# Expert weights in 32 KB runs, two slots of four matrices, and the overflow path ahead of the last four experts

## What is computed

```
# per layer: 32 experts in 4 groups of 8; each token takes the best group and the 2 best experts in it
h2 = modulate(rms_norm(x), shift, scale)
y_e = (silu(h2 @ w_gate[e]) * (h2 @ w_up[e])) @ w_down[e]     # 1024 -> 512 -> 1024, float32
x = x + gate2 * sum over the token's 2 experts of weight * y_e
```

## Time and profile before

| | us |
|---|---|
| median of 3 runs | 2081.34 (2080.13 to 2082.64) |
| the profiled execution, its own time | 2077.69 |
| its span | 2075.9 |
| PE busy, share of the span | 1665.3, 80% |
| DMA, mean rate over the span | 281 GB/s |

### The profile page before, as it was taken

How to read it: one execution, slowest core, us unless ns; L and a number is a source line. 1 busy time by engine, 2 the same in 40 slices (tenths; PEclk the granted TensorE clock), 3 DMA queues, 4 the chain that set the end, 5 groups by cost and what they waited for, 6 DMA issues and landing times.

```text
span 2075.9 us, 26940 instructions
## 1 busy us (share of the span) xinstructions
PE 1665.3 (80%) x12123; PEld 1166.5 (56%) x12123; DVE 521.1 (25%) x931; ACT 323.4 (16%) x641; POOL 50.2 (2%) x79
## 2 busy tenths in 40 slices
PE   8998999999999975565565599999999666565566
PEld 6875877887888832222222188878887222222223
DVE  5776863523101220000000035231023000000001
ACT  2332313212211110000000142211001000000001
POOL 0011100100000000000000001000000000000000
PEclk9999999999999987887887899999999887787787
DMA  7798835204347489999999922134473999999995
GB/s 256 257 350 326 317 150 193 82 3 162 122 162 289 157 337 428 427 427 428 425 424 428 376 94 83 43 122 162 148 302 118 424 427 428 428 427 425 426 427 210
DMA packets 107975, 582.39 MB, mean 281 GB/s; under 512 B 13496, under 2 KB 16336, under 8 KB 83152
## 3 DMA queue, kind: packets, MB, share of 16 engines
q1 hardware_dynamic: 92560, 530.17, 63.3%
q0 software_dynamic: 13056, 50.33, 6.4%
q10 hardware_dynamic: 2240, 0.11, 0.1%
HBM read 579.54 MB, written 1.05 MB: 280 GB/s over the span
## 4 chain that ended last, share of the span: by engine, by line
PE 59%; DMA 23%; DVE 1%; ACT 1%; issue 1%
PE ps L2470 21%; PE ps L1316 13%; PE ps L2104 8%; DMA more_slots<-in_w_exp_up 5%; DMA ring<-in_w_exp_down 4%; DMA more_slots<-in_w_exp_down 4%; PE ps L2117 4%; DMA more_slots<-in_w_exp_gate 4%; DMA ring<-in_w_exp_gate 3%; DMA ring<-in_w_exp_up 3%; PE ps L2142 3%; PE ps L1319 1%; PE ps L1772 1%; PE ps L1784 1%; PE ps L1534 1%; PE ps L1790 1%
## 5 line engine op out<-in xcount | busy, mean ns | idle before, releaser
L2470 PE MATMUL ps<-more_slots,gathered 128*32 128x512 f32 x1184 | 286.7, 718 | 137.9 <-DMA ring<-in_w_exp_up 62.4
L2470 PE MATMUL ps<-ring,gathered 128*32 128x512 f32 x864 | 235.7, 731 | 118.8 <-DMA more_slots<-in_w_exp_up 78.2
L1316 PE MATMUL ps<-h,ring 128*128 128x256 f32 x1216 | 275.5, 382 | 0.0
L1316 PEld LDWEIGHTS ps<-h,ring 128*128 128x128 f32 x1216 | 227.5, 190 | 37.0 <-issue 4.5
L2568 DVE TENSOR_TENSOR gate_up_rows<-silu_rows,ps 128x512 f32<-128x512 f32 x16 | 11.0, 688 | 791.0 <-PE ps L2470 791.0
L2470 PEld LDWEIGHTS ps<-more_slots,gathered 128*32 128x32 f32 x1184 | 70.3, 129 | 247.2 <-issue 246.9
L2470 PE MATMUL ps<-more_slots,gate_up_turned 128*32 128x512 f32 x608 | 147.3, 740 | 70.0 <-DMA ring<-in_w_exp_down 54.1
L2470 PEld LDWEIGHTS ps<-ring,gathered 128*32 128x32 f32 x864 | 56.9, 131 | 208.7 <-issue 208.7
L2104 PE MATMUL ps<-h,ring 128*128 128x256 f32 x768 | 166.7, 379 | 0.0
L2470 PE MATMUL ps<-ring,gate_up_turned 128*32 128x512 f32 x416 | 128.5, 741 | 36.4 <-DMA more_slots<-in_w_exp_down 36.4
L2104 PEld LDWEIGHTS ps<-h,ring 128*128 128x128 f32 x768 | 145.9, 190 | 19.8
(11 more groups left out here) (470 smaller groups left out, 1824.0 us busy)
## 6 DMA issues: line engine op xcount, KB each, us to landing
more_slots<-in_w_exp_gate SPq DMA_DIRECT2D x40, 2048.0 KB, 18.1
more_slots<-in_w_exp_down SPq DMA_DIRECT2D x38, 2048.0 KB, 17.0
more_slots<-in_w_exp_up SPq DMA_DIRECT2D x34, 2048.0 KB, 15.2
ring<-in_w_in SPq DMA_DIRECT2D x31, 2048.0 KB, 9.1
ring<-in_w_exp_up SPq DMA_DIRECT2D x30, 2048.0 KB, 14.6
ring<-in_w_exp_down SPq DMA_DIRECT2D x26, 2048.0 KB, 15.2
ada_ring<-in_w_ada POOLq DMA_DIRECT2D x48, 1024.0 KB, 7.4
ring<-in_w_exp_gate SPq DMA_DIRECT2D x24, 2048.0 KB, 17.8
```

The lines of the kernel that those rows point to most:

```text
L1316: ins = nc.tensor.matmul(k.ps[:, IN_BANK[t], 0:S], slab[:, j, c:c + w], k.h[:, j, :], start=j == 0, stop=j == ND - 1)
L2470: ins = nc.tensor.matmul(k.ps[r, bank, :], left[:, j, r], slab[:, j, c0:c0 + 512], start=j == 0, stop=j == steps - 1)
```

## The change

1. **Layout.** The host stores the gate and up matrices as (layer, partition, expert, 4096), and the down matrices as (layer, column half, partition, expert, 2048). A load takes half a group, 4 MB, with 32 KB on each partition in one run: two experts of gate or up (neighbouring partitions lie 512 KB apart in memory), or one column half of all four downs (256 KB apart).
2. **Slots.** Two slots of four slabs (`expert_slots`, 64 KB per partition each) take the place of seven single ones. Group `g` waits until group `g - 2` is used. One gate slab and the whole up group are loaded ahead of `w_o`, the other three gate slabs as the ring comes free; the ring lies in the upper part of one expert slot. So eight slabs are there before the first group is used.
3. **Downs by column parts.** The left half has its own loads to wait for (`loaded`), the right half a semaphore of its own (`down_right`).
4. **Router weights by quads.** `weigh` (two DVE instructions of 128 columns) multiplies a quad's selection in place, PE turns it with two transposes (`turn_weights`), DVE copies it.
5. **The general path** is called ahead of quad 7 on all four engines, on SP ahead of group 21, and rebuilt (`rest_loads`, `rest_products`, `rest_activations`, `rest_sums`). The function table for the next norm is loaded behind the last SiLU.

```diff
-        for s in range(MORE):
-            load_expert(s)
+        load_gate(0)
+        for part in range(2):
+            load_half(1, part)
         for i in range(N_MIX - 2, N_MIX):
             left(i - SLOTS)
             load(i)
-        for i, s in enumerate(RING_ORDER):
+        for i in range(SLOTS):
             left(N_MIX - SLOTS + i)
-            load_expert(s)
-        for s in range(E_SLOTS, N_SLABS):
-            sp.wait_ge(sem.slabs_used, past.slabs_used + (s - E_SLOTS) // QUAD + 1)
-            load_expert(s)
+            load_gate(1 + (N_MIX * (l + 1) + i) % SLOTS)
+        for g in range(2, N_GROUPS):
+            if g == N_GROUPS - 3:
+                rest_loads(k, y, sp)
+            sp.wait_ge(sem.groups_used, past.groups_used + g - 1)
+            for part in range(2):
+                load_half(g, part)
...
+            if q == N_QUAD - 1:
+                rest_products(k, y, pe)
...
             pe.wait_ge(sem.gu_t_ready, past.gu_t_ready + q + 1)
-            four(1, gu_t, s + 2 * QUAD, 0, N_F).then_inc(sem.down_done, 1)
-            four(0, gu_t, s + 2 * QUAD, 512, N_F).then_inc(sem.slabs_used, 1)
-            if q == 0:
-                pe.wait_ge(sem.scatter_ready, past.scatter_ready + 2)
+            loaded(3 * q + 2)
+            four(1, gu_t, down[:, 0], 0, N_F).then_inc(sem.down_done, 1)
+            pe.wait_ge(sem.down_right[l], 16 * (q + 1))
+            four(0, gu_t, down[:, 1], 0, N_F).then_inc(sem.groups_used, 1)
+            pe.wait_ge(sem.scatter_ready, past.scatter_ready + q + 1)
             scatter_rows(q)
...
             nc.scalar.activation(act_buf[:, :], k.ps[:, 0, :], ACT.Silu).then_inc(sem.act_done, 1)
+            if q == N_QUAD - 1:
+                nc.scalar.preload_act_table_set("natural_log_exp_and_others")
...
         for i in range(SLOTS):
             if l:
-                sp.wait_ge(sem.slabs_used, past.slabs_used - (i < SLOTS - 1))
+                sp.wait_ge(sem.groups_used, past.groups_used - 1)
             load(i)
...
-            remaining_experts(k, y, block)
```

More of the change, by code:

```diff
@@ L1196, in first_block, with expert_rows, group_slot @@
     k.clear(one + ring)
[L1199 to L1218, removed]
+N_GROUPS = 3 * N_QUAD
+def expert_rows(io, l, q, n, part):
+    if n < 2:
+        rows = io[("w_exp_gate_2", "w_exp_up_2")[n]][l, :, q * QUAD + 2 * part:q * QUAD + 2 * part + 2, :]
+    else:
+        rows = io["w_exp_down_2"][l, part, :, q * QUAD:(q + 1) * QUAD, :]
+    return rows.rearrange("p e c -> p (e c)")
+def group_slot(k, g):
+    return k.slots[:, (g + 1) % 2, :]
 N_IN = 11
@@ L2196, in _ @@
                                 ).then_inc(sem.token_sum, 1)
[L2199 to L2209, removed]
-    loaded = (rest.gate_loaded, rest.up_loaded, rest.down_loaded)
[L2212 to L2236, removed]
-            for t in range(NT):
[L2238 to L2252, removed]
@@ new lines, in rest_products @@
+def rest_products(k, y, pe):
+    nc, sem, past, rest = k.nc, y.sem, y.past, y.sem.rest[y.l]
+    h2, gu = k.h2, k.rest_gu
+    loaded = (rest.gate_loaded, rest.up_loaded, rest.down_loaded)
+    with overflow(k, y, pe):
+        pe.wait_ge(sem.rows_left, past.rows_left + N_QUAD)
+        pe.wait_ge(sem.rows_right, past.rows_right + N_QUAD)
+        for t in range(NT):
+            ins = nc.tensor.transpose(k.ps[:, 0, t * P:(t + 1) * P], k.rest[:, t, :], k.const("ident"))
+        ins.then_inc(rest.products, 1)
+        pe.wait_ge(rest.sums, 1)
+        for j in range(ND):
+            for t in range(NT):
+                ins = nc.tensor.transpose(k.ps[:, j // 2, (2 * (j % 2) + t) * P:(2 * (j % 2) + t + 1) * P],
+                                          k.h2_tok[:, t, j, :], k.const("ident"))
+        ins.then_inc(rest.products, 1)
+        with pe.Fori(0, N_E) as e:
+            pe.wait_ge(rest.sums, e * 2 + 2)
+            for n in range(2):
+                pe.wait_ge(loaded[n], e * 16 + 16)
+                slab = k.ring[:, n, :].rearrange("p (j c f) -> p j f c", j=ND, f=N_F)
@@ L2253, in _ @@
                 for f in range(N_F):
                     for j in range(ND):
[L2255 to L2271, removed]
@@ new lines, in rest_products @@
+                        ins = nc.tensor.matmul(k.ps[:, 2 * n + f // 2, f % 2 * S:(f % 2 + 1) * S],
+                                               slab[:, j, f, :], h2[:, j, :], start=j == 0, stop=j == ND - 1)
+            ins.then_inc(rest.products, 1)
+            pe.wait_ge(rest.sums, e * 2 + 4)
+            pe.wait_ge(loaded[2], e * 32 + 32)
+            slab = k.ring[:, 2, :].rearrange("p (b f j c) -> p b f j c", b=2, f=N_F, c=P)
+            for f in range(N_F):
+                for j in range(ND):
+                    ins = nc.tensor.matmul(k.ps[:, 4 + j // 2, j % 2 * S:(j % 2 + 1) * S],
+                                           slab[:, j // 4, f, j % 4, :], gu[:, f // 2, f % 2, :],
+                                           start=False, stop=True, skip_group_check=True)
@@ L2425, in router_rest @@
     step(nc.vector.tensor_tensor(weight[:, :, :], chosen[0][:, :, :], chosen[1][:, :, :], ALU.add))
-    last = lambda a: a.rearrange("p (e o) -> p e o", o=1).broadcast_to([P, N_E, CAP])
-    dve.wait_ge(sem.picked, past.picked + N_QUAD)
-    for t in range(NT):
-        ins = nc.vector.tensor_tensor(k.pick_w[:, t, :, :], k.pick[:, t, :, :], last(weight[:, t, :]), ALU.mult)
     dve.wait_ge(sem.zeros, past.zeros + 2)
@@ L2559, in take_rows, with weigh @@
             ins.then_inc(sem.rows_left, 1)
+        def weigh(q):
+            es = slice(q * QUAD, (q + 1) * QUAD)
+            for t in range(NT):
+                by = k.weight[:, t, es].rearrange("p (e o) -> p e o", o=1).broadcast_to([P, QUAD, CAP])
+                ins = nc.vector.tensor_tensor(k.pick[:, t, es, :], k.pick[:, t, es, :], by, ALU.mult)
+            ins.then_inc(sem.weighted, 1)
         take_rows(0)
```

220 lines of the change are left out of this document (130 added, 90 removed).

## The result

The changed kernel takes 2049.64 us (median of 4 runs, 2048.19 to 2051.91), the one before 2081.77 beside it (4 runs, 2080.13 to 2082.64): ratio 0.985, 95% interval 0.9836 to 0.9863. That is 32.1 us less. The forecast was 2049.8.

What follows compares the result with a forecast made beforehand. Expert phases were taken as bound by their DMA transfers. Terms 9.8 (slabs), 7.0 (downs), 8.2 (branch) make 25.0 us, 31.5 with the rate's 6.5: from the median 2081.3 to 2049.8 us, range 2040 to 2066.

Steps and rivals of the forecast that it cites:

- What bounds the kernel: Both expert phases: each lasts as long as its transfers; PE's speed counts only before the first release and behind the last landing.
- One slab fewer, 4.9 us a layer: Expert phases: eight slabs loaded ahead instead of seven, so 88 follow the first release; 9.8 us less in all.
- All three covers: Time to spare before one slab fewer costs anything: gate group's load 6.6 us, `w_o` slab 8.3, SP's issuing some 10.
- at most 9.52 us: Expert stream: longest a group's use was said to take behind its landing, against 19.7 us of streaming by the next group.
- The branch ahead of quad 7: The flag's branch before the last quad of experts: priced at nothing, at most a few us if a passage took over 10.
- The rate, 6.5 us of 0 to 13: Expert stream: 32 KB runs instead of 16 KB raise 427 GB/s to 430.2, 6.5 us less; bounds 0 and 13.
- The rival with wide steps: Expert stream: wide steps in memory lower the rate, slower than before; 2098.9 us at 407 GB/s; chance 0.10.
- Downs by column parts, 7.0: Behind each phase's last landing: 8 steps of down products instead of 16, 3.5 us less a layer, 7.0 in all.
- The branch, 6.8 and 1.4: Behind the experts: without the flag's branch PE follows the scatter at once, 6.8 us less between layers, 1.4 at program's end.
- its removal adds nothing once the branch is gone: Function table load (1.28 us, twice) behind the experts: lies beside PE's wait, so removing it was said to win nothing more.
- The rival that said code: Layer's end: PE lacks code and stalls anyway beside three slabs; 8.2 us less won, 2058.0 or 2064.5; chance 0.12.
- The low end, 2040: Lower end of the forecast range: 6.5 us more from the rate, up to 4.0 from a clock that stays up.

## Why the prediction was right, by its own steps

- **What bounds the kernel.** Right. Layer 1 up to its first gate group, 396 us with nothing of the change in it, is the same to 0.01 us; everything won lies in the phase's length and behind the landing.
- **One slab fewer, 4.9 us a layer.** Right: 5.0 a slab where two were put back. All three covers held. The gate group's first record follows the gather with no wait for a load, and PE takes the `w_o` slab at 686.75 straight behind the row ahead of it. The stream shows no gap. One reading was off: "at most 9.52 us" is the largest of the rows shown, and the trace of before has up to 10.06; after has up to 10.00, well within the 19.7 us of a group. The branch ahead of quad 7 lies in a wait for the gate group and cost nothing. In after:

```profile
1133.41 8.46 PE L2466 MATMUL ps<-expert_slots,gathered 128*32 128x512 f32 x64 [12.18 <-DMA expert_slots<-in_w_exp_gate]
```

- **The rate, 6.5 us of 0 to 13.** Right in size: two points, 2 and 16 KB, gave 430.2 GB/s for 32, and 430 came. With 16 KB put back 3.4 and 3.2 us return. That the cost goes by the run and not by the load is argued from the 2 KB row, not shown by itself. The rival with wide steps, priced by the nearest poor row, fell with a layout that has no such steps and the same rate.
- **Downs by column parts, 7.0.** The mechanism was right, the term too large for these executions: 5.9 between the traces, 5.3 with the edit taken back alone. The eight steps fewer are worth their 3.5 us. What was mis-sized is the slow start: it was kept at 2.3 + 1.7 = 4.0 us as if it were fixed, and it was 2.4 + 2.6 = 5.0 in after and 1.4 + 2.0 = 3.4 with whole downs. It varies from 1.3 to 3.0 from landing to landing in long and short rows alike, with the same mean of 2.1, so one landing a layer can't be forecast to better than about 1 us. The idle time was put at "some 3 us"; its own four terms give 3.7, and it was 4.57 and 4.23.
- **The branch, 6.8 and 1.4.** 7.1 and 1.7 came. For the first, the cause holds: put back alone, the stall returned, and with it a slower stretch behind it (5.50 us for the 18 records, which take 4.05 in after), 6.5 us together. For the second, the size came out by luck and the reason didn't hold: with the branch put back, the end of the program shows no stall. By the chain of before the function table stands there, 1.28 us in front of the squares. If it is the cause, "its removal adds nothing once the branch is gone" fails at the end of the program. That edit was not run alone, so this is argued and not shown.
- **The rival that said code** was right on what PE lacks as far as the runs can tell, and wrong on the outcome: with the plain branch and three slabs in flight at 374 GB/s there was no stall.
- **The range.** Its ends, 10 us below and 16 above, were not needed: rate and slabs together came 0.3 us above their terms and the branch 0.6, and only the downs were off, by 1.1 to 1.7. That the sum was met to 0.2 us (31.3 of 31.5) is luck: the downs fell short by about what the others gave beyond their terms, and the first block alone moves an execution by more. The low end, 2040, wanted a clock that stays up, which needed nine matmuls more and gave 4.6 to 5.0 us.

## What to carry to other kernels

Where a phase is a stream at the rate of the DMA engines, write it as (what lies behind the first release) / rate + (what PE must do behind the last landing), and attack the two ends: release the first slot from the middle of a group, and let the last load be the smallest with PE kept busy up to it. The two ends gave some 15 us here, and longer runs 2, when the rate had less than 1% left to give. Put a conditional long path where the engines wait for a transfer anyway, never between two dependent rows that run beside one, and take the slow start behind a wait as a spread (1.3 to 3.0 us here for waits of 3.4 us and more) and not as one value.

## What the runs showed of the hardware that was not expected

- PE can stall behind a conditional jump in the middle of a row, 10 records in: 3.67 us, beside transfers at 315 GB/s over the stretch around it; none at 12 GB/s; none at the program's end.
- The same 32 records took 3.57 to 3.64 us where PE had been kept busy and 4.93 to 6.46 behind 3.4 to 4.9 us of idle time, and the longer time doesn't go with the longer wait: 6.45 us behind 4.01, 5.34 behind 4.93. Behind 1.97 and 1.98 us they took 5.34 and 3.64.
- Reads with neighbouring partitions 256 and 512 KB apart run at the same 430 GB/s as contiguous ones.
- Behind the first block, the same in all thirteen kernels, the first projection of layer 0 starts anywhere from 333.04 to 338.59 us in their traces, over 5 us apart, so two spans should be compared by stages and not by their ends.
